# Constant products in four waits of TensorE around the expert stage, and the last layer norm by sums on ScalarE and moments on GpSimd

## What is computed

```
x = layer_norm(ALPHA * x + m[:, 2] * (mixed @ w_out), ln_g[0], ln_b[0])
h = modulate(x, m[:, 3], m[:, 4])
y = moe_ffn(h, w_router, router_bias, wg, wu, wd)      # two of 16 experts for each token
x = layer_norm(ALPHA * x + m[:, 5] * y, ln_g[1], ln_b[1])

layer_norm(x, g, b): mu = mean(x); var = mean((x - mu) ** 2)
                     (x - mu) * rsqrt(var + LN_EPS) * g + b
```

## Time and profile before

| | |
|---|---|
| median of 3 runs | 2099.53 us (2098.99 to 2108.22) |
| the profiled execution | 2098.44 us, of which its span 2096.6 us |
| PE busy | 1805.8 us, 86% of the span |
| DVE, ACT, POOL busy | 767.8, 374.2, 309.9 us |
| mean granted clock of PE | 0.94 |
| matmul by line, busy | L855 769.9 us, L583 365.3 us, L815 140.3 us, L574 140.4 us |

### The profile page before, as it was taken

The page is one execution under the profiler, slowest core; times in us unless marked ns, Lnnn a source line. Parts: engine busy times, 40 slices in busy tenths (PEclk is TensorE's granted clock), DMA queues, the critical chain, the costliest instruction groups (busy, mean ns, idle before and its releaser), DMA issues. The chain is left out here.

```text
span 2096.6 us, 20602 instructions
## 1 busy us (share of the span) xinstructions
PE 1805.8 (86%) x7528; PEld 926.9 (44%) x7528; DVE 767.8 (37%) x1179; ACT 374.2 (18%) x695; POOL 309.9 (15%) x348
## 2 busy tenths in 40 slices
PE   3999998788965999999799999787788399999983
PEld 1464554555443443434346445454544243443431
DVE  0035577374562110011150566646636311101105
ACT  1322142243010000000141223213410000000002
POOL 0013453000000000000130254310000000000005
PEclk9999999899976999999999999998999599999996
DMA  9421111565019787799603012126120696797933
GB/s 366 146 102 41 42 42 46 192 241 201 20 50 346 265 315 291 285 361 390 228 18 136 7 40 84 46 96 250 43 90 30 239 348 234 295 367 290 395 127 150
DMA packets 142086, 380.43 MB, mean 181 GB/s; under 512 B 9732, under 2 KB 15876, under 8 KB 135332
## 3 DMA queue, kind: packets, MB, share of 16 engines
q1 hardware_dynamic: 111840, 292.31, 37.3%
q10 hardware_dynamic: 21108, 55.36, 7.4%
q0 software_dynamic: 9040, 31.46, 4.1%
HBM read 343.65 MB, written 35.45 MB: 181 GB/s over the span
## 5 line engine op out<-in xcount | busy, mean ns | idle before, releaser
L855 PE MATMUL psum<-sb_arena 128*128 128x512 f32 (+1 forms) x1248 | 494.1, 596 | 10.6 <-DMA sb_arena<-w_up 9.1
L583 PE MATMUL psum<-sb_wA,sb_arena 128*128 128x512 f32 x800 | 365.3, 604 | 0.0
L855 PEld LDWEIGHTS psum<-sb_arena 128*128 128x128 f32 (+1 forms) x1248 | 192.5, 171 | 269.7 <-issue 257.7
L855 PE MATMUL psum<-sb_wA,sb_arena 128*128 128x512 f32 (+1 forms) x672 | 275.8, 607 | 9.0 <-DMA sb_wA<-w_up 6.3
L583 PEld LDWEIGHTS psum<-sb_wA,sb_arena 128*128 128x128 f32 x800 | 147.5, 192 | 164.1 <-issue 158.1
L1328 DVE TENSOR_TENSOR sb_arena<-sb_arena 128x320 f32<-128x320 f32 (+8 forms) x252 | 179.1, 752 | 15.5 <-POOL sb_arena L1264 6.1
L1848 DVE COPY sb_arena<-psum 128x1024 f32<-128x1024 f32 x32 | 39.2, 1225 | 344.3 <-PE psum L843 344.3
L855 PEld LDWEIGHTS psum<-sb_wA,sb_arena 128*128 128x128 f32 (+1 forms) x672 | 102.3, 169 | 118.3 <-issue 108.0
L1494 DVE COPY_PREDICATED sb_arena<-sb_masks,psum 128x640 f32<-128x640 uint8 x128 | 112.3, 877 | 94.5 <-PE psum L656 75.1
L574 PE MATMUL psum<-sb_arena,sb_wA 128*128 128x128 f32 (+1 forms) x512 | 140.4, 435 | 0.0
L815 PE MATMUL psum<-sb_wA,sb_arena 128*128 128x512 f32 x320 | 140.3, 599 | 0.0
(11 more groups left out here) (185 smaller groups left out, 1684.4 us busy)
## 6 DMA issues: line engine op xcount, KB each, us to landing
sb_arena<-w_gate SPq DMA_DIRECT2D x22, 2048.0 KB, 18.7
sb_arena<-w_down SPq DMA_DIRECT2D x22, 2048.0 KB, 15.6
sb_wA<-w_up SPq DMA_DIRECT2D x16, 2048.0 KB, 20.0
sb_arena<-w_up SPq DMA_DIRECT2D x16, 2048.0 KB, 16.1
sb_wA<-w_ada SPq DMA_DIRECT2D x13, 2048.0 KB, 7.7
sb_wA<-w_in SPq DMA_DIRECT2D x12, 2048.0 KB, 9.5
sb_arena<-w_ada SPq DMA_DIRECT2D x11, 2048.0 KB, 7.6
sb_wA<-w_gate SPq DMA_DIRECT2D x10, 2048.0 KB, 18.1
```

What stands on the lines that cost most here:

```text
L583: mm = pe.matmul(unit_bank(n), hT[:, k, t * P:(t + 1) * P], w[:, k, :], start=k == 0, stop=k == KD - 1)
L855: mm = pe.matmul(out[r, :], act_T[:, k, r], w[:, k, cs], start=k == 0, stop=k == kn - 1)
```

## The change

Four calls of a new function `stay_warm(b, n)` stand in TensorE's program of each layer. It multiplies the identity by the first 512 columns of the constants, n times, into a PSUM bank that nothing reads there (bank 2); nothing waits for it. The calls: six products after the router and ahead of the wait for `m_ready`; eleven after the ranks, ahead of `at_ready`; eight after the token list, ahead of the first block's rows; five after the last block, ahead of the overflow loop.

The last norm of the second layer gets its mean and variance from two sums that ACT forms (a Copy and a Square of the tile with an accumulated output, into scrap space), POOL turns these into mean, variance, reciprocal root and bias in six small operations with drains between them, ACT normalises, and DVE does both the product with `ln_g` and the sum with `ln_b`. DVE does this for a tile two tiles later (`final(t - 2)` after `residual(t)`). In the first layer the norm stays, but for the place of the wait for `ln2_in`.

```diff
--- before.py
+++ after.py
@@ -273,6 +273,9 @@
+        sum1, sum2 = Z[:, 0:NT], Z[:, NT:2 * NT]
+        fine = [cc[:, 0:1], cc[:, 1:2]]
+        scrap = [view(o_, 1024) for o_ in (0, 1024, 2048, 3072, 4096, 5120, 6144, 7168, 10240, 14592)]
...
@@ -511,6 +514,11 @@
+            def stay_warm(b, n):
+
+                for _ in range(n):
+                    pe.matmul(bank(b), ident, cst[:, 0:W], start=True, stop=True)
+
...
@@ -820,10 +828,12 @@
                 router(NT - 1)
 
+                stay_warm(2, 6)
                 pe.wait_ge(m_ready, l + 1)
...
+                stay_warm(2, 11)
                 pe.wait_ge(at_ready, l + 1)
...
@@ -873,6 +883,7 @@
+                stay_warm(2, 8)
                 tokens_in(0)
...
@@ -885,6 +896,7 @@
                 outputs(NBK - 1)
 
+                stay_warm(2, 5)
                 until(pe, pos_ready, l + 1)
...
@@ -1193,8 +1205,15 @@
                 if l + 1 == DEPTH:
-                    for t in range(NT):
-                        normalise(l, t)
+                    for t in range(NT + 1):
+                        if t < NT:
+                            act.wait_ge(last_x, t + 1)
+                            act.activation(scrap[2 * t], x[:, t, :], ACT.Copy, accum_out=sum1[:, t:t + 1])
+                            act.activation(scrap[2 * t + 1], x[:, t, :], ACT.Square, accum_out=sum2[:, t:t + 1]).then_inc(sums_ready, 1)
+                        if t:
+                            act.wait_ge(rstd_ready, nth(l, N_VAR, 2 + 2 * NT + t))
+                            act.activation(x[:, t - 1, :], x[:, t - 1, :], ACT.Identity, bias=nmr[:, t - 1:t],
+                                           scale=rstd[:, t - 1:t]).then_inc(centred, 1)
...
@@ -1310,14 +1329,25 @@
-                until(gp, ln2_in, l * 32 + 32)
-                for t in range(NT):
-                    until(gp, var_ready, nth(l, N_VAR, 3 + 2 * NT + t))
-                    gp.tensor_tensor(rstd[:, t:t + 1], mv[:, t, 1:2], mhalf[:, 0:1], ALU.pow).then_inc(rstd_ready, 1)
-                    if t and l + 1 == DEPTH:
-                        add_shift(l, t - 1)
-                if l + 1 == DEPTH:
-                    add_shift(l, NT - 1)
...
+                else:
+                    for t in range(NT):
+                        c1 = slice(t, t + 1)
+                        until(gp, sums_ready, t + 1)
+                        gp.tensor_scalar(nmean[:, c1], sum1[:, c1], -1.0 / D, None, ALU.mult)
+                        gp.tensor_scalar(fine[0], sum2[:, c1], 1.0 / D, EPS, ALU.mult, ALU.add)
+                        gp.drain()
+                        gp.tensor_tensor(fine[1], nmean[:, c1], nmean[:, c1], ALU.mult)
+                        gp.drain()
+                        gp.tensor_tensor(fine[0], fine[0], fine[1], ALU.subtract)
+                        gp.drain()
+                        gp.tensor_tensor(rstd[:, c1], fine[0], mhalf[:, 0:1], ALU.pow)
+                        gp.drain()
+                        gp.tensor_tensor(nmr[:, c1], nmean[:, c1], rstd[:, c1], ALU.mult).then_inc(rstd_ready, 1)
...
@@ -1876,13 +1906,28 @@
                 until(v, m5_in, l * 16 + 16)
+                until(v, ln2_in, l * 32 + 32)
+
+                def residual(t):
+                    v.wait_ge(cmb_mm, nth(l, NT, t + 1))
+                    dr_()
+                    tt(ysum, psum[:, (t % 2) * 1024:(t % 2) * 1024 + 1024], gate_mod[:, 0 if t == 0 else 1, :]).then_inc(cmb_used, 1)
+                    dr_()
+                    return stt(x[:, t, :], x[:, t, :], ALPHA, ysum, ALU.mult, ALU.add)
+
+                def final(t):
+                    v.wait_ge(centred, nth(l, NT, t + 1))
+                    tt(x[:, t, :], x[:, t, :], lnb2[:, 0, :])
+                    dr_()
+                    tt(x[:, t, :], x[:, t, :], lnb2[:, 1, :], ALU.add).then_inc(x_ready, 1)
+
                 for t in range(NT):
...
+                    if l + 1 == DEPTH:
+                        residual(t).then_inc(last_x, 1)
+                        if t >= 2:
+                            final(t - 2)
+                        continue
...
-                    if t == 0:
-                        until(v, ln2_in, l * 32 + 32)
-                    elif l + 1 == DEPTH:
-                        v.wait_ge(centred, nth(l, NT, t))
-                        times_g(l, t - 1)
                 if l + 1 == DEPTH:
-                    v.wait_ge(centred, nth(l, NT, NT))
-                    times_g(l, NT - 1)
+                    final(NT - 2)
+                    final(NT - 1)
```

More of the change, by code:

```diff
@@ L300, in build_program @@
         x_in, consts, lam_in = sem("x_in"), sem("consts"), sem("lam_in")
-        cst_in, nmr_ready, mod_tr, modc_ready = sem("cst_in"), sem("nmr_ready"), sem("mod_tr"), sem("modc_ready")
+        cst_in, last_x, sums_ready, nmr_ready, mod_tr, modc_ready = sem("cst_in"), sem("last_x"), sem("sums_ready"), sem("nmr_ready"), sem("mod_tr"), sem("modc_ready")
         bias_in, cond_in, cond_zero = sem("bias_in"), sem("cond_in"), sem("cond_zero")
@@ L1311, in _ @@
                                               bass.IndirectOffsetOnAxis(ap=posi[:, t, q:q + 1], axis=0)).then_inc(cmb_in[t], 16)
-                until(gp, ln2_in, l * 32 + 32)
-                for t in range(NT):
-                    until(gp, var_ready, nth(l, N_VAR, 3 + 2 * NT + t))
-                    gp.tensor_tensor(rstd[:, t:t + 1], mv[:, t, 1:2], mhalf[:, 0:1], ALU.pow).then_inc(rstd_ready, 1)
-                    if t and l + 1 == DEPTH:
-                        add_shift(l, t - 1)
-                if l + 1 == DEPTH:
-                    add_shift(l, NT - 1)
+                if l + 1 < DEPTH:
+                    until(gp, ln2_in, l * 32 + 32)
+                    for t in range(NT):
+                        until(gp, var_ready, nth(l, N_VAR, 3 + 2 * NT + t))
+                        gp.tensor_tensor(rstd[:, t:t + 1], mv[:, t, 1:2], mhalf[:, 0:1], ALU.pow).then_inc(rstd_ready, 1)
+                else:
+                    for t in range(NT):
+                        c1 = slice(t, t + 1)
[10 more added lines that the diff above has]
+                        gp.tensor_tensor(nmr[:, c1], nmean[:, c1], rstd[:, c1], ALU.mult).then_inc(rstd_ready, 1)
         @block.vector
@@ L1878, in _ @@
                 until(v, m5_in, l * 16 + 16)
-                for t in range(NT):
-                    y = 0 if t == 0 else 1
-                    dr_()
-                    v.wait_ge(cmb_mm, nth(l, NT, t + 1))
-                    tt(ysum, psum[:, (t % 2) * 1024:(t % 2) * 1024 + 1024], gate_mod[:, y, :]).then_inc(cmb_used, 1)
-                    dr_()
-                    stt(x[:, t, :], x[:, t, :], ALPHA, ysum, ALU.mult, ALU.add)
+                until(v, ln2_in, l * 32 + 32)
[10 more added lines that the diff above has]
+                    tt(x[:, t, :], x[:, t, :], lnb2[:, 1, :], ALU.add).then_inc(x_ready, 1)
+                for t in range(NT):
+                    if l + 1 == DEPTH:
[3 more added lines that the diff above has]
+                        continue
+                    residual(t)
                     dr_()
```

## The result

The changed kernel takes 2084.92 us in the median of four runs (2083.03 to 2086.89), the kernel before 2099.8 in four runs beside it. The ratio is 0.9924, 95% interval 0.9902 to 0.9945: 14.9 us by the medians, and more than half a percent over the whole interval. The profiled execution took 2086.89 us, span 2085.1, mean granted clock 0.958 (before: 2098.44, 2096.6 and 0.940). Forecast were 2087.4 and a gain of 12.1.

The account below looks back on a forecast made before the run. Bound: TensorE's waits around the experts and the lower-clock steps between them, then the last norm's three-engine chain. 2 x 4.3 + 0 + 3.5 = 12.1 us off 2098.44 gives 2086.3, or 2087.4 on the median's footing; range 2080.5 to 2094.5.

Parts of the forecast that it names:

- What bounds, and the ideal: Around the experts, short steps behind TensorE's waits run on the path at the lower clock; ideal gain 6.4 us per layer.
- Cover: The first three calls, 7.3 to 8.3, 9.7 and 7.0 us, fit waits of 9.79, 12.12 and 8.71 us.
- The remainder: Idle 1.5 to 2.5 us behind each of the first three calls risks clock falls; 4.3 of 6.4 us remain per layer.
- Does it reach the end?: In the expert stages, weight loads follow TensorE's slot releases, so the gain of 4.3 us per layer is not swallowed.
- rival (d): Expert weights come too late for an earlier start, only the last norm's gain stays: 2096.0 us; chance 0.06.
- The fourth call: After the last expert product, the clock falls again before combining: gain 0, between 0 and a loss of 1.0 us per layer.
- The last norm: At the program's end, the second layer's new norm over DVE, POOL and ACT gains 3.5 us.
- (a): The clock falls in the idle time behind each of the first three calls: gain 7.9 us, 2091.6; chance 0.12.
- (b): The clock never falls behind the calls and POOL is not held up: gain 19.8 us, 2079.7; chance 0.12.
- (c): POOL's chain becomes the bound of the last norm, a loss of 3.5 us there: 2094.4 us; chance 0.14.
- (e): Products of constants do not raise TensorE's clock, so the calls end late: slower, 2123 us; chance 0.04.
- (f): Turns do not count as work for the clock, so it falls before the first expert product: 2089.1 us; chance 0.05.

## Why the prediction was right

The time (2087.4 forecast, 2084.9 measured) and the sign came out, on the steps that it named; two of its sizes were off, in the same direction. The three edited stretches give 16.3 us by the traces for the 12.1 of the forecast; that the whole traces differ by 11.5, so near to 12.1, is luck, since draws outside the edits took the rest back.

- **What bounds, and the ideal.** 6.4 us a layer were to be had, 5.7 were had; of the rest 0.6 and 0.3 us went to the first block's rows, which land 9.5 and 9.0 us behind the list's end for 8.9 and 8.7 before, and 0.3 in the second layer to the list. Left out one at a time, the third call is worth 3.0 us a layer (3.9 forecast for the turn and the first product) and the second 1.8 (2.0).
- **Cover.** Right, with 7.5 us for the first call (7.3 to 8.3). The second and third took 11.3 and 8.5 for 9.7 and 7.0, because the falls landed in them (second layer), and the waits still covered them.
- **The remainder: the step that failed.** I put half of 4.2 us a layer at risk behind the calls and took 4.3 for 5.7. The falls came as often as I took (three in six; over the ten kernels 31 in 60), but I put their price on the steps behind the idle time. My price came from blocks of 24 products, 14 us long, on which a fall must land; behind the first two calls the steps are 0.5 to 2.7 us and the next call stands behind each, so the fall reached constants. Behind the third call, where no call follows, I put 1.7 us at risk and no fall came in twenty layers; why not, no run shows. One layer in twenty paid in full; in others the list lost up to 0.3.
- **Does it reach the end?** Yes. Waits for weights in the second layer's experts are 8.0 us for 7.1; rival (d) is out.
- **The fourth call.** 0, as forecast; the loop's 6.44 us lie between the 3.8 and 7.9 of the estimate.
- **The last norm.** 4.9 us for 3.5, by two errors against each other. The first tile's final operations begin 12.2 us after the first combined tile, not 10.2: the first drain's 2.95 us was in no row of before. From there to the end it is 20.1 us, not 23.4: POOL's small operations pass between DVE's, a tile takes 5.08 us and not 5.3 to 5.8, and the last two 3.9 or less.
- **Rivals.** (a) is refuted in its price, since falls behind the calls cost next to nothing, (e) by the second layer's rows, (f) by the turns. (b) is nearest for the calls. (c) was not the case but near: a chain of six operations leaves POOL 2.4 us a tile, one of eleven is the bound. The rule on the shared interface (the Trainium skill, "GPSIMD Engine Reference", Key points) agrees with the trace, 0.19 to 0.57 us against 1.02 to 1.36; what I couldn't price is that POOL alone pays, with DVE's operations at 1.22 to 1.25 throughout.

## What to carry to other kernels

Where TensorE waits and its clock falls, products of constants into a bank that nothing reads pay, if the step behind is on the path, the call ends before the wait does, and little of the wait is left behind the call (up to 2.9 us did, in all but one case; the 7.0 us behind the fourth call did not). Put one ahead of each short step, since a fall that comes late then lands on the next call. A group without a wait in front is no proof that TensorE is the bound there: making it faster may only uncover the wait of another engine a little behind. Before small operations are moved to GpSimd beside VectorE, count how many of them fall under operations with two SBUF inputs, and keep the chain short enough to pass in between.

## What the runs showed of the hardware

- GpSimd's first drain behind ten gathers took 2.95 us when it began 7.3 to 9.0 us after the last one's issue, with all ten landed (eleven kernels), and 6.80 when it began about 1.3 us after; later drains leave gaps of 0.15.
- A small GpSimd operation under a VectorE operation with two SBUF inputs lasts until that has ended: plain ones end within 0.1 us of it (1.02, 1.10 and 1.21 us for 0.19 to 0.22), a power about 0.4 after it (1.36 for 0.57). By the Trainium skill, "SBUF — State Buffer", SBUF: two separate sides, the loser of the shared ports waits out the other's whole instruction; the rows agree for GpSimd.
- Turns alone raise TensorE's clock: 0.50 to the upper level within a call of 7.02 us.
- TensorE's loop of eight turns that do nothing, with the reading of its count, takes 6.44 us, and the clock falls in it.
